# The recurrence of a two-block network: the first half of an inverse begins one step later in its round

## What is computed

```python
def step(S, inp):
    r_t, w_t, k_t, v_t, kk_t, a_t = inp
    sa = jnp.einsum("bhvk,bhk->bhv", S, kk_t)
    S = (S * w_t[:, :, None, :]
         - sa[..., None] * (kk_t * a_t)[:, :, None, :]
         + v_t[..., None] * k_t[:, :, None, :])
    return S, jnp.einsum("bhvk,bhk->bhv", S, r_t)
```

## Time and profile before

| | us |
|---|---|
| median of 3 runs | 2547.51 (2538.16 to 2547.98) |
| the profiled execution | 2544.79 |
| its span, first to last instruction | 2542.9 |
| mean granted clock of TensorE, as a share of full speed | 0.938 |

### The profile page before, as it was taken

One profiled execution on the slowest core, in us unless ns is written; L12 is line 12 of the kernel. 1 busy time (PEld: TensorE's weight loads), 2 busy tenths in 40 slices (PEclk: granted clock), 3 DMA queues, 4 the chain that ended last, 5 costly groups with the idle time before them and its releaser, 6 DMA issues.

```text
span 2542.9 us, 59404 instructions
## 1 busy us (share of the span) xinstructions
PE 2170.9 (85%) x25764; PEld 1622.8 (64%) x25764; DVE 1361.8 (54%) x2326; ACT 1152.3 (45%) x1933; POOL 678.8 (27%) x410
## 2 busy tenths in 40 slices
PE   8799999289888988886689999996889987898888
PEld 2587777167766766775567666663666665666666
DVE  1357878434444454454336666664356663466752
ACT  2466666233333333343235455543355553355552
POOL 0334453300001011011333222222434332433332
PEclk9899999599999999999899999997999998999998
DMA  7115453642432222212213111110222221222222
GB/s 264 66 58 173 132 161 110 195 131 78 115 90 80 64 63 58 71 43 108 96 58 108 50 44 53 54 50 31 101 75 83 67 67 63 70 77 78 63 67 67
DMA packets 156164, 221.37 MB, mean 87 GB/s; under 512 B 84481, under 2 KB 109313, under 8 KB 155137
## 3 DMA queue, kind: packets, MB, share of 16 engines
q1 hardware_dynamic: 144800, 174.32, 22.6%
q0 software_dynamic: 9952, 40.11, 5.2%
q10 hardware_dynamic: 1152, 3.15, 0.3%
HBM read 164.84 MB, written 42.21 MB: 81 GB/s over the span
## 4 chain that ended last, share of the span: by engine, by line
PE 59%; DVE 15%; ACT 11%; issue 8%; POOL 4%; DMA 2%; SPq 0%; ACTq 0%; DVEq 0%; POOLq 0%
PE ps L257 8%; PE ps L259 7%; PE ps L258 7%; PE ps L1337 3%; PE ps L543 3%; PE ps L1327 2%; PE ps L1352 2%; PE ps L2253 2%; PE ps L396 2%; PE ps L2790 2%; PE ps L2213 1%; PE ps L2767 1%; ACT p L2273 1%; DVE pc L2856 1%; DVE s L921 1%
## 5 line engine op out<-in xcount | busy, mean ns | idle before, releaser
L242 POOL TENSOR_TENSOR wbl<-wb,wbh 128x1024 fp32r<-128x1024 f32 x128 | 308.6, 2411 | 639.2 <-ACT wbh L237 635.4
L257 PE MATMUL ps<-hTh,wah 128*128 128x512 f32 (+1 forms) x512 | 181.0, 354 | 17.5 <-POOL wal L242 11.1
L257 PE MATMUL ps<-hT2h,wbh 128*128 128x512 f32 x416 | 180.2, 433 | 10.6 <-POOL wbl L242 10.3
L258 PE MATMUL ps<-hTl,wah 128*128 128x512 f32 (+1 forms) x512 | 175.2, 342 | 0.0
L259 PE MATMUL ps<-hTh,wal 128*128 128x512 f32 (+1 forms) x512 | 174.9, 342 | 0.0
L257 PE MATMUL ps<-hT1h,wbh 128*128 128x512 f32 (+1 forms) x432 | 168.5, 390 | 3.1 <-POOL hT1l L2394 3.1
L344 POOL TENSOR_TENSOR ro<-ro 128x256 f32<-128x256 f32 (+1 forms) x12 | 11.9, 994 | 583.9 <-DVE ro L328 583.9
L237 ACT ACTIVATE wbh<-wb 128x1024 fp32r<-128x1024 f32 x128 | 134.6, 1052 | 69.3 <-PE ps L1933 43.3
L259 PE MATMUL ps<-hT2h,wbl 128*128 128x512 f32 x416 | 164.6, 396 | 0.0
L258 PE MATMUL ps<-hT2l,wbh 128*128 128x512 f32 x416 | 164.0, 394 | 0.0
L242 POOL TENSOR_TENSOR wal<-wa,wah 128x1024 fp32r<-128x1024 f32 x34 | 102.5, 3015 | 219.3 <-ACT wah L237 219.3
(11 more groups left out here) (411 smaller groups left out, 5609.3 us busy)
## 6 DMA issues: line engine op xcount, KB each, us to landing
wb<-in_w_in SPq DMA_DIRECT2D x56, 512.0 KB, 3.5
s_str_dram<-s POOLq DMA_DIRECT2D x48, 576.0 KB, 8.7
wm<-in_ada SPq DMA_DIRECT2D x48, 512.0 KB, 4.5
bkv<-s_str_dram SPq DMA_DIRECT2D x96, 192.0 KB, 3.4
wa<-in_rw_in SPq DMA_DIRECT2D x34, 512.0 KB, 3.7
wb<-in_da_in SPq DMA_DIRECT2D x32, 512.0 KB, 3.5
ARI<-s_str_dram SPq DMA_DIRECT2D x96, 128.0 KB, 3.5
wb<-in_w_out SPq DMA_DIRECT2D x16, 512.0 KB, 3.5
```

Source lines behind the costliest of these rows:

```text
L242: e.tensor_tensor(self.lo[:, n % 2], self.raw[:, n % 3], self.hi[:, n % 2].bitcast(F32), ALU.subtract).then_inc(self.K.s.w_lo, 1)
L257: e.matmul(z, wh[:, k, :], hi[:, k, a:b], start=k == 0, stop=False)
L258: e.matmul(z, wh[:, k, :], lo[:, k, a:b], start=False, stop=False)
```

## The change

The first half of the inverse of unit u+2 gets an empty step ahead of its eight, and its number of steps for the pace is 9 instead of 8. It does the same eight steps as before. The rounds 0 to 21 have such a part. Nothing else is changed.

```diff
-        def inverse(u, n):
-            if u not in inverts:
-                inverts[u] = invert(u)
-            return some(inverts[u], n), n
+        def inverse(u, n, behind=0):
+
+            def steps():
+                for _ in range(behind):
+                    yield
+                if u not in inverts:
+                    inverts[u] = invert(u)
+                yield from some(inverts[u], n)
+            return steps(), n + behind
@@
             if u + 2 < 24:
-                parts.append(inverse(u + 2, 8))
+
+                parts.append(inverse(u + 2, 8, 1))
```

## The result

The changed kernel takes 2552.05 us (median of 20 runs) beside 2544.02 us for the kernel before (20 runs); the ratio is 1.0033, with a 95% interval of 1.0021 to 1.0045. That is +8 us (5 to 11; brackets behind a ratio or a difference are this interval throughout): slower, but by less than half a per cent, and 13 us less than the 21.8 forecast. The profiled execution has a span of 2554.9 us against 2542.9. From the first C1 to the last C1 the recurrence takes 643.1 us against 633.3, so 9.8 of these 12 us lie where the change is.

A forecast was written before the change was run, and what follows sets the result against it. The prediction took TensorE's work and waits to bound the kernel. Its terms, -3 + 0 + 18.8 + 0.6 + 2.4 + 7 - 4 = +21.8 us, counted from 2547.5, gave 2569 us, range 2550 to 2587.

The forecast's parts named there:

- The order, the holes and their causes: Recurrence rounds: step order before and after, a 1.76 us mid-round TensorE hole from VectorE's queue, other waits shifted.
- The middle, 15 x 1.25: Middle of 15 rounds without a readout: TensorE waits for a masked copy queued on VectorE, 1.25 us each, +18.8 us.
- The clock behind the middle hole, +7: After the new mid-round hole TensorE gets half clock in 4 spells over 15 rounds: +7 us, bounds 0 and +25.
- The start after a readout, -3 - 4: Starts of six rounds after a readout: moved steps fill the wait, -3 us; less low clock, -4 us.
- rival 2: Round's start outweighs the middle: whole 22.5 us wait and 13 us of low clock saved; 2533 us, or 2519; chance 0.11.
- The start in the other rounds, 0: Starts of rounds not following a readout: wait short or already hidden, so 0 us, bounds -3 and +3.
- the readout rounds: Six rounds with a readout: small delays in the middle and front, 0.4 us each, +2.4 us.
- the rounds 21 and 22: End of the recurrence: only round 21, which has no preparation, was given a loss, +0.6 us.
- (1): Delay swallowed: later holes shrink in about half of 15 rounds, -9 us, no new clock spells; 2553 us, chance 0.17.
- (3): A low-clock spell behind the middle hole in every one of the 15 rounds, +25 for +7; 2587 us, chance 0.08.

The follow-up runs named there:

- middle_only: Kernel before with only the middle changed: first two steps of the first half of the inverse as before, other six at 4/9 to 9/9; 2560.49 us, ratio 1.0062.
- after_tail: Changed kernel's order, with the last part of a readout on VectorE moved into the next round as in tail_before; 2541.02 us, ratio 0.9994 to the kernel before.
- tail_middle: middle_only with the last part of a readout on VectorE moved as in tail_before; 2539.20 us, ratio 0.9993 to the kernel before.
- late_only: Changed kernel's order from round 6 on, the order of the kernel before in rounds 0 to 5; 2538.91 us, ratio 0.9979 to the kernel before.
- start_only: Kernel before with only the round's start changed: first two steps of the inverse's first half at 0.2 and 0.3, others as before; 2531.85 us, ratio 0.9957.
- start_post: As start_only, but only in the six rounds that follow a readout, all others as in the kernel before; 2532.26 us, ratio 0.9954.
- fetch_later: Kernel before, but SyncE's eight fetches of a round also wait for the next round's first chain step; 2541.35 us, ratio 1.0005.
- tail_before: Kernel before, but on VectorE the last part of a readout is put into the next round, ahead of the first chain step; 2514.68 us, ratio 0.9896.

## Why the forecast missed

**The order, the holes and their causes** came out as written: both orders, the hole of 1.76 us ahead of B4 (1.80), 15 times, B6's 0.2 us in place of A6's, the wait of A2 behind a readout (1.52), nothing to gain at P7's holes. The sign was right. Of the 13 us that are missing, 7 are the clock behind the middle hole, some 4 the start after a readout and 2 to 3 the middle itself. Costs that had no term or one too small, in the first six and the last two rounds, and a smaller loss in the later plain rounds roughly cancel by the traces; the sum below has them.

**The middle, 15 x 1.25.** A little too large. From C1 to A5 the median plain round takes 8.82 us before and 10.40 after. B2 now stands in this stretch. I had put it at 0.68 us, the start-to-start time of the earlier trace rows; behind C1 it takes only 0.49 (1007.41 to 1007.90), so the round loses 10.40 - 8.82 - 0.49 = 1.09 us. middle_only, where B2 stays ahead of C1, gives it without that step: 9.96 - 8.82 = 1.14. 15 times that is 16 to 17 us, as middle_only measured (16).

**The clock behind the middle hole, +7.** This term failed. I had priced four spells at half the clock; there was none. The traces of the changed kernel and of middle_only have 30 middle holes of 1.80 us, those of after_tail, tail_middle and late_only 39 more, and within 4 us behind none of them does the granted clock fall. A hole of 1.61 us in P7 is followed by 0.57 over the stretch of four us shown above, in the same trace. I had taken the length of a hole as what counts, from two rows that already disagreed with each other. The length alone doesn't decide it. The new hole has levels, preparation and chain packed close on either side, the holes of P7 stand at the end of a round; which part of that decides, no run here varies, so it stays open.

**The start after a readout, -3 - 4.** Half again as large: -11 us by start_only, -12 by start_post. In the trace of start_post the part from A7 to the next C1 is 1.9 us shorter on average. The idle time fell by 0.6 us, near the 0.5 worked out. The other 1.3 are the clock: it is low for 12.1 us in these six stretches where it was low for 27.2, and 15.1 us at half speed cost 7.6, which is 1.3 a round. I had given the clock 0.7 a round there, although rival 2 already priced its whole low time at 13 us.

**The start in the other rounds, 0.** Right in start_only, but not in the changed kernel, whose rounds 0 to 5 lose 8 us to a low clock at their starts that neither half shows alone. I had no term for it. It is about as large as the middle's clock term that did not come, so these two misses cancel each other in the forecast.

**The sum again.** 16 for the plain middles, 1 for the readout rounds (from C1 to A5 the six take 61.0 us before, 62.4 in middle_only; 2.4 were forecast), 3 for the rounds 21 and 22 (39.2 us before, 42.5 after; 0.6 were forecast), -11 for the starts, nothing for the middle's clock: +9. That this is near the measured +8 is in part luck, since the early rounds' 8 us are not in it, and with them it would be +17, above the 11 that the interval allows. The two traces account for the recurrence's 9.8 us like this: +14.7 in the rounds 0 to 5, -12.1 in the six readout rounds with the starts behind them, +3.9 in the nine later plain rounds, +3.3 in the last two. The nine lose their 1.1 us each from C1 to A5 as well and get part of it back behind it, where the holes of P7 are 16.3 us and not 19.8. That difference is no larger than the scatter among the traces, so how much the later plain rounds lose rests on single executions and stays open.

**The rivals.** (1) is out: with the changed middle the holes of P7 are 16.3 to 18.7 us, with the old one 16.4 to 19.8, and fetch_later shows them bound to places in the stream. Its time, 2553, is the measured one all the same, for another reason. (2) had the mechanism of the gain right, low clock and all, and its end at tail_before, not at this change: A2 was held by the readout as the earlier trace rows said. (3), a spell behind every middle hole, is refuted by 69 of 69.

The Trainium skill, "Runtime: NRT & Kernel Launch", section "Instruction fetch mechanics", says that crossing a block of instructions is mostly hidden. By the packets of the instruction queue the trace agrees with "mostly": 17 of 133 are followed by a stop above 0.8 us. But those 17 cost 33.5 us, in P7 1.9 to 4.5 us each. The 2.91 us of the earlier trace rows are one of them: the packet ended at 1044.29, 1.30 us before TensorE went on, so this was no wait that A1 and P1 could cover.

## What to carry to other kernels

When a step is moved to fill a wait, list what it leaves behind as well: the step after it now follows its source without cover, and on every engine that serves it the copies stand in a new order; 1.1 us in 15 rounds ate a gain of 2 us in six. Before filling a wait, ask what it waits for: here two slow operations of VectorE stood ahead of the one awaited and two more ahead of the next copies, and moving these four out of the way gave 26 us where moving the waiting step gave 11. A net of two opposed terms needs each of them to be right, so its range should come from the terms and not from the net.

## What the runs showed of the hardware that was not expected

- A hole of 1.80 us between densely packed steps left the clock at its upper level 69 times of 69, in five traces. Of the 19 holes of 1.48 to 2.91 us without a releaser at the end or the start of a round, in the traces before and after, 14 were followed by the lower level within four us (and 1027 to 1031 above). The mean clock over the span was 0.938 before and 0.939 after, although single rounds moved by several us.
- After a wait of 4.32 us TensorE ran at half the clock for six us; taking such waits away brought back about 10 us in six rounds beyond the 14.5 us of idle time.
- TensorE stops in the middle of a step at fixed places of its instruction stream, and goes on 1.2 to 1.6 us behind a packet of the instruction queue (204 of 204 stops above 0.8 us). With the data fetches of SyncE in flight the seven stops of P7 last 2.3 to 2.8 us on average, with the fetches moved away 1.8.
